# Differential attention in a float32 hybrid block: queries and keys of six heads turned by VectorE squares and DMA instead of TensorE

## The reference

```python
z = rms_norm(x, norm_g) @ w_in                     # 1024 x 9216, split into q_r, k_r, ..., q_d, k_d, v_d, ...
qd = rms_norm(q_d.reshape(B, S, 8, 2, 64), diff_q_norm_g)
kd = rms_norm(k_d.reshape(B, S, 8, 2, 64), diff_k_norm_g)
# per head h and block i of 128 queries, for j = 0, 1:
s_j = (q_j * 64 ** -0.5) @ k_j.T - slope_h * dist  # keys 0 .. 128 (i + 1)
p_j = softmax(where(dist >= 0, s_j, -inf))
o = (p_0 - lam * p_1) @ v
```

## Time and profile before

| | us |
|---|---|
| median of 3 runs | 909.57 |
| lowest, highest | 909.09, 910.21 |
| the profiled execution, whole | 908.68 |
| its span in the trace | 906.9 |
| TensorE busy | 896.1 (99%) |
| VectorE, ScalarE, GpSimd busy | 423.1 (47%), 397.3 (44%), 439.2 (48%) |

### The profile page before, as it was taken

The page is one execution under the profiler, slowest core; times in us unless marked ns, Lnnn a source line. Parts: engine busy times, 40 slices in busy tenths (PEclk is TensorE's granted clock), DMA queues, the critical chain, the costliest instruction groups (busy, mean ns, idle before and its releaser), DMA issues.

```text
span 906.9 us, 12615 instructions
## 1 busy us (share of the span) xinstructions
PE 896.1 (99%) x4648; PEld 712.7 (79%) x4648; DVE 423.1 (47%) x957; ACT 397.3 (44%) x872; POOL 439.2 (48%) x376
## 2 busy tenths in 40 slices
PE   9999999999999999999999999999999998999998
PEld 7878888888888877777777788889888765777776
DVE  3221251545114413467474455646648866543631
ACT  5533323333223344454554444244435774655531
POOL 4544436445446654646444444545458382234362
PEclk9999999999999999999999999999999999999999
DMA  8442222313333332122222233233433321011113
GB/s 317 152 104 77 65 70 79 108 59 105 96 104 100 97 90 73 48 72 70 69 55 63 70 116 139 93 108 96 120 101 105 94 87 53 25 47 47 47 47 116
DMA packets 43564, 81.29 MB, mean 90 GB/s; under 512 B 4416, under 2 KB 6208, under 8 KB 43504
## 3 DMA queue, kind: packets, MB, share of 16 engines
q1 hardware_dynamic: 42016, 79.95, 29.3%
q10 hardware_dynamic: 1488, 0.55, 0.3%
HBM read 78.36 MB, written 2.12 MB: 89 GB/s over the span
## 4 chain that ended last, share of the span: by engine, by line
PE 84%; DVE 8%; issue 3%; POOL 2%; DMA 2%; ACT 1%; SPq 0%; ACTq 0%; DVEq 0%; POOLq 0%
PE Z L1708 23%; PE Z L1710 22%; PE Z L1709 22%; PE A L1885 3%; PE A L1808 2%; PE A L1923 2%; PE A L1894 2%; PE A L1820 2%; DMA raw<-in_w_in 2%; DVE z_sb L1239 1%; PE A L1868 1%; POOL w_lo L943 1%; DVE rstd L1142 1%; PE A L1833 1%; PE A L1718 1%
## 5 line engine op out<-in xcount | busy, mean ns | idle before, releaser
L943 POOL TENSOR_TENSOR w_lo<-raw,w_hi 128x512 fp32r<-128x512 f32 (+1 forms) x262 | 345.3, 1325 | 443.9 <-ACT w_hi L574 442.6
L574 ACT CAST w_hi<-raw 128x512 fp32r<-128x512 f32 (+1 forms) x262 | 157.9, 614 | 293.7 <-PE Z L1710 259.7
L1708 PE MATMUL Z<-w_hi,hT_hi 128*128 128x512 f32 (+1 forms) x544 | 217.8, 400 | 0.1
L1710 PE MATMUL Z<-w_hi,hT_lo 128*128 128x512 f32 (+1 forms) x544 | 211.3, 388 | 0.0
L1709 PE MATMUL Z<-w_lo,hT_hi 128*128 128x512 f32 (+1 forms) x544 | 210.8, 388 | 0.0
L1708 PEld LDWEIGHTS Z<-w_hi,hT_hi 128*128 128x128 f32 x544 | 102.3, 188 | 27.8 <-issue 8.3
L1710 PEld LDWEIGHTS Z<-w_hi,hT_lo 128*128 128x128 f32 x544 | 102.1, 188 | 20.8
L1709 PEld LDWEIGHTS Z<-w_lo,hT_hi 128*128 128x128 f32 x544 | 102.4, 188 | 17.7
L1708 PE MATMUL Z<-hT_hi,w_hi 128*128 128x512 f32 x260 | 113.1, 435 | 0.3 <-DVE hT_lo L1174 0.3
L1710 PE MATMUL Z<-hT_hi,w_lo 128*128 128x512 f32 x260 | 102.1, 393 | 0.0
L1709 PE MATMUL Z<-hT_lo,w_hi 128*128 128x512 f32 x260 | 101.6, 391 | 0.0
(11 more groups left out here) (239 smaller groups left out, 1298.7 us busy)
## 6 DMA issues: line engine op xcount, KB each, us to landing
raw<-in_w_in SPq DMA_DIRECT2D x91, 512.0 KB, 3.8
raw<-in_w_out SPq DMA_DIRECT2D x16, 512.0 KB, 3.6
raw<-in_ret_w_o SPq DMA_DIRECT2D x8, 512.0 KB, 3.2
raw<-in_diff_w_o SPq DMA_DIRECT2D x8, 512.0 KB, 3.3
x_sb<-in_x SPq DMA_DIRECT2D x4, 512.0 KB, 6.0
x_sb<-in_xT SPq DMA_DIRECT2D x4, 512.0 KB, 6.8
out<-x_sb SPq DMA_DIRECT2D x8, 256.0 KB, 2.9
raw<-in_w_in SPq DMA_DIRECT2D x4, 416.0 KB, 3.3
```

The lines of the kernel that those rows point to most:

```text
L574: act.copy(w_hi[:, s % SPLIT_SLOTS, 0:width], raw[:, c % RAW_SLOTS, s - CHUNK_START[c], 0:width]).then_inc(hi_ready, 1)
L943: pool.tensor_tensor(w_lo[:, s % SPLIT_SLOTS, 0:width], raw[:, c % RAW_SLOTS, s - CHUNK_START[c], 0:width], w_hi[:, s % SPLIT_SLOTS, 0:wid ...
L1708: pe.matmul(out, l_hi, r_hi, start=first, stop=False)
L1710: return pe.matmul(out, l_lo, r_hi, start=False, stop=last)
```

## The change

Heads 0 and 4 (`stacked(h)` false) stay as they were, except that the key gain is multiplied into the query gain. For the other six:

- After the norm VectorE transposes the normalised rows in 32x32 squares (`turned_rows`, one instruction of 128x512 for each row tile, 16 in all) into `d_rows`. SyncE writes them to DRAM (`rows_written`, four DMAs for each half of queries and of keys, in pieces of 512 bytes) so that they lie there as 64 rows x 512 columns for each map, and reads them per head twice, into both row halves of `q_raw` or `k_raw` (`read_twice`). Four writes and twelve pairs of reads stand at given slabs in SyncE's queue (`ROWS_OUT`, `QUERIES_IN`, `KEYS_IN`).
- Queries: VectorE multiplies the gain in (`queries_gained`), ScalarE copies to `q_both` in fp32r (high part, reordering columns), VectorE puts the low part in the lower 64 rows (`queries_low`). Keys: ScalarE copies `k_high` in all 128 rows, GpSimd writes `k_low` (`keys_low`).
- Scores: two fp32r matmuls over 128 rows for each map, `q_both` with `k_high` and with `k_low`, in place of one float32 matmul over 64 rows.
- Twelve of the fourteen turn steps in the stage go, so the stage has 74 steps and not 86, and `diff_due` has new bounds. The norms of the second halves have twelve pieces (four block transposes more) in slots 9 to 20 of groups 15 and 16, one a slot. The output norms of heads 0 to 3 go to slabs 0 and 1 of group 18. GpSimd's squares of groups 10 and 11 are made two a slab.

```diff
-DIFF_FIRST, DIFF_SECOND, DIFF_THIRD, DIFF_LAST = 10, 116, 160, 208
+DIFF_FIRST, DIFF_SECOND, DIFF_THIRD, DIFF_LAST = 10, 120, 149, 208
+DIFF_STEPS = 2 * (4 * H + 4) + 2
...
-        return 36 * (v - DIFF_FIRST + 1) // (DIFF_SECOND - DIFF_FIRST)
+        return 33 * (v - DIFF_FIRST + 1) // (DIFF_SECOND - DIFF_FIRST)
     if v < DIFF_THIRD:
-        return 36 + 22 * (v - DIFF_SECOND + 1) // (DIFF_THIRD - DIFF_SECOND)
-    return min(86, 58 + 28 * (v - DIFF_THIRD + 1) // (DIFF_LAST - DIFF_THIRD))
+        return 33 + 9 * (v - DIFF_SECOND + 1) // (DIFF_THIRD - DIFF_SECOND)
+    return min(DIFF_STEPS, 42 + (DIFF_STEPS - 42) * (v - DIFF_THIRD + 1) // (DIFF_LAST - DIFF_THIRD))
...
+ROWS_OUT = (0, 8, 28, 36)
+QUERIES_IN = {1: 4, 2: 14, 3: 20, 5: 32, 6: 40, 7: 44}
+KEYS_IN = {1: 10, 2: 16, 3: 22, 5: 38, 6: 42, 7: 46}
...
+            def rows_written(i):
+
+                v = qk_dram[:, :, :]
+                sp.wait_ge(rows_ready, TT * (i + 1))
+                for q in range(4):
+                    to = bass.AP(tensor=v.tensor, offset=(16 * i + 4) * 32 * S + P * q, ap=[[S, 32], [32 * S, 12], [1, P]])
+                    rows = d_rows[32 * q:32 * (q + 1), 4:16, :, :].rearrange("r b t c -> r b (t c)")
+                    sp.dma_start(to, rows).then_inc(rows_out, 16)
...
+            def keys_read(h):
+
+                half, w = divmod(h, 4)
+                sp.wait_ge(rows_out, 64 * (2 * half + 2))
+                if h > 1:
+                    sp.wait_ge(k_lo, 2 * stacked_number(h))
+                read_twice(k_raw, 2 * half + 1, w, k_in)
...
+                    if i == 1 and h + 1 < H and stacked(h + 1):
+                        queries_high(h + 1)
+                    if i == 2 and h + 1 < H and stacked(h + 1):
+                        keys_high(h + 1)
...
+            def keys_low(h):
+
+                for j in range(2):
+                    pool.wait_ge(k_hi, 2 * stacked_number(h) + j + 1)
+                    slot = diff_slot_of(h, j)
+                    pool.tensor_tensor(by_squares(k_low[:, slot, :]), in_order(k_raw[:, j, :]),
+                                       by_squares(k_high[:, slot, :]), ALU.subtract).then_inc(k_lo, 1)
...
+            def turned_rows(c0, i, t):
+
+                dve.wait_ge(head_normed, TT * i + t + 1)
+                if i and t == 0:
+                    dve.wait_ge(rows_out, 64 * i)
+                dve.transpose(d_rows[:, :, t, :], z_sb[:, t, c0:c0 + 512].rearrange("p (b c) -> p b c", c=32)
+                              ).then_inc(rows_ready, 1)
...
+                    if i == 2 and h + 1 < H and stacked(h + 1):
+                        queries_low(h + 1)
...
+                    if i == 0 and h + 1 < H and stacked(h + 1):
+                        queries_gained(h + 1)
...
+            def queries_gained(h):
+
+                dve.wait_ge(q_in, 32 * (stacked_number(h) + 1))
+                dve.tensor_scalar(q_raw[:, :, :], q_raw[:, :, :], cols[:, 35:36], None, ALU.mult).then_inc(q_gained, 1)
+
+            def queries_low(h):
+
+                low = slice(DK, P)
+                for j in range(2):
+                    dve.wait_ge(q_hi, 2 * stacked_number(h) + j + 1)
+                    q = by_squares(q_both[low, diff_slot_of(h, j), :])
+                    dve.tensor_tensor(q, in_order(q_raw[low, j, :]), q, ALU.subtract).then_inc(q_lo, 1)
...
-                    if normed_in(g) and k in (3, 4):
+                    if normed_in(g) and 9 <= TT * k + t <= 20:
                         next(norms[g])
-                    if g == G_DIFF0 + 4 and k in (5, 6):
+                    if g == G_DIFF0 + 5 and k in (0, 1):
                         next(norms["first"])
...
-                    pe.wait_ge(qk_out, 2 * h + 2)
+                    if stacked(h):
+                        pe.wait_ge(q_lo, 2 * stacked_number(h) + 2)
+                        pe.wait_ge(k_lo, 2 * stacked_number(h) + 2)
+                    else:
+                        pe.wait_ge(qk_out, h // 2 + 2)
...
+                            if stacked(h):
+                                slot = diff_slot_of(h, j)
+                                q = q_both[:, slot, P * i:P * (i + 1)]
+                                pe.matmul(bank, q, k_high[:, slot, keys], start=True, stop=False)
+                                pe.matmul(bank, q, k_low[:, slot, keys], start=False, stop=True).then_inc(s_mm, 1)
```

More of the change, by code:

```diff
@@ L271, in build @@
         m_sb = sb("m_sb", [P, TT, D], F32)
+        with ExitStack() as scope:
+            sb("d_rows", [P, 4, S], F32R, scope)
+            k_low = sb("k_low", [P, 4, S], F32R, scope)
         sgd_sb = sb("sgd_sb", [P, KD, S], F32)
@@ L275, in build @@
                           for v in (m_sb, x_sb, o_sb))
+        with ExitStack() as scope:
+            q_both = sb("q_both", [P, 4, S], F32R, scope)
+            k_high = sb("k_high", [P, 4, S], F32R, scope)
         qT = sb("qT", [P, 4, S], F32)
@@ L525, in _ @@
                     sp.wait_ge(row_out, 16)
+                for i in range(4):
+                    if SLAB0[g] + k - SLAB0[G_DIFF0] == ROWS_OUT[i]:
+                        rows_written(i)
+                for h in range(H):
+                    if stacked(h) and SLAB0[g] + k - SLAB0[G_DIFF0] == QUERIES_IN[h]:
+                        queries_read(h)
+                    if stacked(h) and SLAB0[g] + k - SLAB0[G_DIFF0] == KEYS_IN[h]:
+                        keys_read(h)
                 if g == G_DIFF_OUT + 1 and k == 0:
@@ L1240, in head_scale, with head_norm @@
                                       ALU.mult).then_inc(head_normed, 1)
+                for t in range(TT if rows is not None else 0):
+                    yield
+                    turned_rows(c0, rows, t)
                 yield
-            def head_norm(c0, squares, turns):
+            def head_norm(c0, squares, turns, rows):
                 for t in range(TT):
@@ L1249, in head_norm @@
                         turned(cT_lo[:, k, :], cT_hi[:, k, :], cols[:, 32 + k:33 + k])
-                for _ in head_scale(c0):
+                for _ in head_scale(c0, rows):
                     pass
@@ L1440, in diff @@
                     yield
-                    if i in (1, 2) and h + 1 < H:
+                    if i in (1, 2) and h + 1 == H // 2:
                         yield
+                    if i == 0 and h + 1 < H and stacked(h + 1):
+                        queries_gained(h + 1)
                     yield
+            def queries_gained(h):
[3 more added lines that the diff above has]
+                low = slice(DK, P)
+                for j in range(2):
+                    dve.wait_ge(q_hi, 2 * stacked_number(h) + j + 1)
+                    q = by_squares(q_both[low, diff_slot_of(h, j), :])
+                    dve.tensor_tensor(q, in_order(q_raw[low, j, :]), q, ALU.subtract).then_inc(q_lo, 1)
             def diff_slot(g, k, steps, norms):
@@ L1806, in scores @@
                         for j in range(2):
-                            rows = slice(DK * j, DK * (j + 1))
-                            pe.matmul(A[j][:, score_columns(i, True)], qT[rows, h % 2, P * i:P * (i + 1)],
-                                      kT[rows, h % 2, 0:P * (i + 1)], start=True, stop=True).then_inc(s_mm, 1)
+                            bank, keys = A[j][:, score_columns(i, True)], slice(0, P * (i + 1))
+                            if stacked(h):
[3 more added lines that the diff above has]
+                                pe.matmul(bank, q, k_low[:, slot, keys], start=False, stop=True).then_inc(s_mm, 1)
+                            else:
+                                rows = slice(DK * j, DK * (j + 1))
+                                pe.matmul(bank, qT[rows, 0, P * i:P * (i + 1)], kT[rows, 0, keys],
+                                          start=True, stop=True).then_inc(s_mm, 1)
                 def outputs(m):
```

83 lines of the change are left out of this document (66 added, 17 removed).

## The result

| | before | after |
|---|---|---|
| median, us (lowest to highest) | 909.4 (909.1 to 910.2) | 918.2 (917.1 to 919.6) |
| the profiled execution, its span | 908.7, 906.9 | 919.6, 917.8 |
| ratio to before, 95% interval | | 1.0096 [1.0079, 1.0114] |

A forecast was written before the change was run, and what follows sets the result against it. TensorE's issue time was taken as the bound (busy 99%). 10.4 us gained less 9.1 of waits gave 1.3 less than 908.7, so 907.4; the median 0.9 above that, 908.3, range 901.5 to 914.

The forecast's parts named there:

- TensorE's gain: Differential stage: 5.4 us of turns and 20.1 of score groups removed, 15.1 of matmuls added; 10.4 us gained, ends 7.7 and 11.3.
- the rival of four passes: 128-column matmuls take 0.22 us, not 0.11, costing 2.7 us of the gain; 1.4 us slower, 911.0; chance 0.10.
- Block 11's scores: Group 15, slot 83: TensorE waits 1.1 to 2.6 us for VectorE's maxima of block 10, taken as 1.2.
- the root: VectorE's inverse root in group 15's norm: 2.1 + 3.1 = 5.2 us, or 4.7 with one instruction not held up.
- Block 12's scores: Group 15, slot 89, head 3: TensorE waits 2.4 to 5.5 us for VectorE's maxima of block 11, taken as 2.5.
- The key turn: Group 16, slot 113, head 4's second key turn: wait 3.3 to 4.7 us, 0.9 before; 2.3 more taken.
- Slots 156 to 171: Around block 23: maxima 1.7 to 2.2 us late, keys 3.4 late; wait 1.7 to 5, taken as 3.1.
- 10.4 gained, 9.1 lost: Whole kernel: TensorE's gain less four waits, 1.2 + 2.5 + 2.3 + 3.1, for 1.3 us less.
- Weight transfers: Weight chunks behind the new row writes and reads: hidden, put at nothing; without cover 1 to 3 us.
- Waits covered: Rival: three of the four waits shrink to nothing, 2 to 4 us left, 902.2; chance 0.25.
- VectorE held up: Rival: two-input VectorE instructions wait out GpSimd's; four more hold-ups of 1.1 us, waits 13.5, time 912.7; chance 0.20.
- Does what it says: Rival that it doesn't: score groups' cost lies in the group change; at most 0.3 a head, 1.6 us; no own chance.

The follow-up runs named there:

- experiment 4: The changed kernel without GpSimd's subtractions of the keys' low parts for heads 3, 5, 6 and 7; 915.4 us, ratio 1.0068.
- experiment 2: The changed kernel with the output norms of heads 0 to 3 moved from group 18 to group 19; 913.1 us, ratio 1.0042.
- experiment 1: The changed kernel with 20, 30 and 32 extra matmuls of 256 columns right ahead of TensorE's three long waits; 913.9 us, ratio 1.0057.
- 5: The changed kernel with group 15's block transposes, head 4's second key turn and the output norms later, keys' low parts one step earlier; 905.4 us, ratio 0.9956.
- experiment 3: The changed kernel with group 15's four block transposes moved behind block 11's maxima and their row write two slabs later; 916.9 us, ratio 1.0081.
- 6: The changed kernel with the new DRAM tensor declared ahead of the two small ones; 916.9 us, ratio 1.0088.
- 8: The changed kernel with the second key turn of head 4 in slot 119, not 113; 911.9 us, ratio 1.0030.
- 10: The kernel of experiment 5 with group 15's last two scalings behind block 11's maxima and head 4's second key turn in slot 121; 902.5 us, ratio 0.9930.
- 12: The kernel of experiment 10 with group 15's last two scalings in slot 94, behind block 12's maxima; 901.9 us, ratio 0.9926.

## Why the prediction was wrong, point by point

*TensorE's gain*: 10.4 forecast, 10.2 measured. The 0.11 for 128 columns, the one choice in it, holds; the rival of four passes falls.

*Block 11's scores* (1.2 forecast): no wait, the maxima were done 0.3 us ahead. The term that was mis-sized here is the root, 5.2 by the rows of before and 3.7 here: one of its instructions was held up (1.2), not two. Rows of a root that ran beside other GpSimd work do not carry over.

*Block 12's scores* (2.5): 2.60. The lower end of that term adds up to 7.1 and not 7.6, which takes the transposes at 0.68 and not at the 0.55 given; they took 0.62. *The key turn* (3.2 with before's 0.9, just under its own ends of 3.3 to 4.7): 4.20. *Slots 156 to 171* (3.1, ends 1.7 to 5): 4.10 + 0.9 = 5.0, at the upper end. Here the maxima were 4.1 late where I had 1.7 to 2.2; three root instructions of 0.17 took 1.2 each (experiment 4). The keys were 2.6 late (experiment 2), not 3.4. Idle time in all 12.4 where 10.0 was counted: 2.4 of the miss.

*The step that failed* is the sum itself: "10.4 gained, 9.1 lost" counts a wait at its idle time. Before had no wait over 0.9 us in the stage, so none of its rows showed what comes after a long one, and the text has no term for it and no bound. It was 7.4 us, and about 6 of them are the clock (my estimate from the jobs above: 2.9 at block 12, 1.6 behind the turn, 1.5 at block 24); experiment 1 gave back 4.3 by keeping TensorE busy. With it the same forecast of the waits gives 908.3 + 7.4 = 915.7, a loss. The Trainium skill ("TensorE: Matmul & The Clock Gate", "HAM oscillation — how this bites in real kernels") describes waits for the data of DMAs between groups of matmuls that bring TensorE back to its low clock, and the trace agrees, here with waits on VectorE (a granted clock of 0.57 in 396 to 402 us). I had weighed its page on packing and not this one.

*Weight transfers* (nothing): right in the stage, where no wait on weights came up. The 2.1 us arose more than 150 us behind the last of the change's transfers, where I had not looked.

*The rivals.* Waits covered: no. VectorE held up: the mechanism is there (experiments 4, 5): three root instructions of the output norms, one in each root of groups 15 and 16 and one scaling in each sat behind GpSimd. It gave 912.7, nearest of all, and lacked the same two terms. *Does what it says*: yes.

## What to carry to other kernels

When a change trades work of the bounding engine for waits, price each wait at its idle time plus the low clock behind it, and ask first whether the waits can be moved: here the same change is worth +8.8 us or -7.7 by the order alone in which the pieces stand on the engines' queues. Put long-lead work of a half-idle engine behind the instruction that TensorE waits for, not ahead of it, and check at each move which GpSimd instruction runs beside it then. A step moved from one consumer's path lands on the next one's (experiment 3), so follow the queue to the engine behind it.

## What the runs showed of the hardware that I had not expected

- After waits of 4.1 us and more the granted clock was at its lower level in every trace that had them (after, experiments 2, 3, 4, 6 and 8). After waits of 2.2 to 2.6 us at block 12 it was at the lower level in four kernels (after, 4, 5, 6) and full in two (2, 8); after, 2, 6 and 8 do the same work in the same order up to there. So it is with waits for weights in the second layer: low after 2.0 us (10), full after 2.1 (12) and 2.2 (after). The fall came 0.7 us before TensorE went on at block 12 (396.8) and 1.0 us after it at the key turn (427.6). What decides this was not tried; at block 12 it is worth 2.9 us.
- TENSOR_SCALAR instructions of 128x16 elements, 0.17 us each, took up to 1.26 beside a GpSimd instruction, and scalings with two inputs 1.78 instead of 0.68. Block transposes (0.6 each) and the maxima did not, though GpSimd's subtractions ran beside them. Those at block 12 took 1.48 each and not the 1.24 of block 24; the transposes are not the reason, for they took 1.49 in experiment 3, where the transposes stand elsewhere.
- A write of 2 KB on ScalarE's queue took 9.5 us to land in the second layer, and 12.3 when 40 DMAs had been issued on another queue more than 150 us before. In the first layer, with none before it, it took 10.8 to 12.4.
